# State-space scan in a two-block model: where in the program, and into which PSUM bank, each group's scores are written

## The chip, the cores and the metric

The kernel runs on one core of a Trainium2 chip. Its time is the device time of one execution in microseconds (us). A core has a matrix engine (TensorE, "PE" in the profile, with its weight loads as "PEld"), a vector engine (VectorE, "DVE"), a scalar engine (ScalarE, "ACT"), a slower general engine (GpSimd, "POOL") and a queue that issues transfers (SyncE, "SP"). Each engine works through its own instructions in the order of the program and meets the others only at semaphores. TensorE writes its results into PSUM, a memory of eight banks of 128 x 512 fp32 values; the other memory on the core is SBUF.

## The reference, cut to what matters

Two blocks of a language model are computed one after the other for 256 positions of width 1024. The second block begins with a state-space mixer of 32 heads in 8 groups of 4, head width 64, state width 128. The change is inside its scan, which in the reference is this:

```python
def ssd_chunked_scan(xs, dt, A, Bm, Cm):
    ...
    def step(state, inp):
        xc, dtc, bc, cc = inp
        cum = jnp.cumsum(dtc * A, axis=1)
        seg = cum[:, :, None] - cum[:, None, :]
        decay = jnp.exp(jnp.where(causal, seg, -jnp.inf))
        cb = jnp.einsum('btgn,bsgn->btsg', cc, bc)          # one set of scores for each group
        w = cb[..., None] * decay * dtc[:, None]            # one set of weights for each head
        y = jnp.einsum('btsgk,bsgkp->btgkp', w, xc)
        ...
```

Around the scan stand an input projection (of which the gate z is a part), a short convolution, and behind it a gate, a norm for each group and an output projection:

```python
SSD_N_HEADS, SSD_N_GROUPS, SSD_D_STATE, SSD_HEAD_DIM = 32, 8, 128, 64
zxbcdt = x @ in_proj
z = zxbcdt[..., :SSD_D_INNER]                               # 256 x 2048
```

The kernel does not carry a state between two chunks of 128: it computes the scores, the decay and the sum over all 256 positions at once, as the lower triangle of three 128 x 128 tiles (384 columns, `TRI`).

## The kernel before, in words

**Matrix products.** Every weight matrix comes in units of 1 MB (128 x 2048 fp32). SyncE loads a unit into one of five slots of `raw`; ScalarE rounds it into `whi` (L774), VectorE forms the rest `wlo` (L1201), and TensorE computes each product as three: high by high (L1938), high by low (L1939), low by high (L1940). A unit's slot is free again when TensorE has gone through it (`unit_used`).

**The stage of the scan.** It has 16 units: eight of the gate's projection (`zz`, two for each quarter of 512 columns) and eight of the output projection (`so`). Each unit is cut into four steps (`SSD_PER_UNIT`), so that there are 64 steps. In `a_unit` the function `between(n)` is called ahead of each step, and then six matmuls of 128 x 512 of the unit follow. What else belongs to a step is in the table `SSD_STEPS`: "head" h, "norm" and "yT" of a quarter of eight heads, "tail", or nothing. Heads 0 to 7 are steps 4 to 11, heads 8 to 10 steps 12 to 14, head 11 step 17, "yT" 0 is step 19, heads 12 to 18 are steps 20 to 26, head 19 is step 29, "yT" 1 step 31, head 20 step 32, head 27 step 41, "yT" 2 step 43, heads 28 to 31 steps 44 to 47, and "yT" 3 step 55.

**One head.** SyncE loads the head's row of cumulated decay into one of four buffers (`dec`, three of which lie in `arena`; `decay_row`, L641) once TensorE has finished head h - 4 (the semaphore `ssd_y`). GpSimd adds the causal mask (L735), ScalarE takes the exponential (L1026, L1027), VectorE multiplies it with the scores of the head's group in PSUM (L1745; "multiply h" below), and two steps later TensorE multiplies the product with the head's input (L2440 to L2442; "sum h" below) into the banks 2 and 3.

**The scores.** `ssd_scores` (L2429, L2430) computes a group's scores, two matmuls, at the step of the first of its four heads (0, 4, 8, ...), behind sum h - 2 and ahead of the step's six matmuls. All groups use bank 1. `claim` lets TensorE wait until the bank's last reader is done with it. For a group that is the multiply of the fourth head of the group before; where a "yT" lies between, it is that one's last reader.

**A quarter of eight heads.** When sum 8q + 7 is done, VectorE adds the banks 2 and 3 to y (L1700), multiplies with the gate (L1708), takes statistics (L1714, L1717), GpSimd the inverse root (L682), VectorE scales (L1725, "norm"). At "yT" TensorE transposes the quarter's y, eight transposes into two banks (L2460): the first half (j = 0) into bank 0 and the second (j = 1) into bank 1. ScalarE reads them (L801) and rounds them into `r_hi`, VectorE reads them (L1233) and forms `r_lo`, and the last of VectorE's reads of a half frees its bank. At a step with n = 3, VectorE's own list has the forming of a unit's `wlo` (L1201) ahead of what else the step holds, "yT" included.

**What sets the order.** All of this is written out by hand. The function `plan` walks through the same steps and notes for each use of a bank (`small`, `gemm`, `named`) which use came before it there; the waits of `claim`, `wait_bank` and `wait_drained` are made from it. VectorE's and ScalarE's lists (from L1728 and L1010) follow the same table `SSD_STEPS`.

Of the kernel before, what the change touches and what calls it, by code (L numbers as in the profile page):

```python
# [40 lines left out]
P = 128  # L41
T = 256
# [17 lines left out]
TRI = 3 * P  # L60
# [5 lines left out]
SSD_UNITS, SSD_PER_UNIT = 16, 4  # L66


def ssd_steps():

    steps = [("none", 0)] * SSD_PER_UNIT
    for h in range(SSD_HEADS):
        steps.append(("head", h))
        if h % 8 == 2 and h > 8:
            steps += [("none", 0), ("norm", h // 8 - 1)]
        if h % 8 == 3 and h > 8:
            steps += [("none", 0), ("yT", h // 8 - 1)]
    steps.append(("tail", SSD_HEADS))  # L80
    steps += [("none", 0)] * (SSD_PER_UNIT * (SSD_UNITS - 2) - 1 - len(steps)) + [("yT", 3)]
    return steps + [("none", 0)] * (SSD_PER_UNIT * 2)


SSD_STEPS = ssd_steps()


def group_order(groups):
# [119 lines left out]
def plan(w):  # L208

    p = Plan()  # L210
    w_in = w["w_in"][0]
    p.transposes("h1", 4, (4, 5, 6, 7))
    SQ, SK, SV, RET, CB, CC, CH, GATE = (MIX * j for j in (3, 4, 5, 6, 0, 1, 2, 10))
# [135 lines left out]
    for u in range(SSD_UNITS):  # L349
        c, k = u // 2, u % 2  # L350
        if c < 4:
            p.unit(("zz", c, k), w_ssd, 4 * k, 4, 512 * c, 512)
        else:
            p.unit(("so", c - 4, k), w["ssd_out_proj_2"][0], 4 * (c - 4), 4, 512 * k, 512)
        for what, h in SSD_STEPS[SSD_PER_UNIT * u:SSD_PER_UNIT * (u + 1)]:
            if what == "head":
                if h % 4 == 0:
                    p.small(("CB", h // 4), 1)
            if h % 8 == 7 and what != "yT":
                for t in range(NT):  # L360
                    p.named(("y", h // 8, t), 2 + t, "ssd_y", h + 1)
            if what == "yT":
                for b in range(2):
                    p.small(("yT", h, b), b)
        if u == 0:
            p.small(("xsN", 7), 5)
        if c < 4 and k == 1:
            for t in range(NT):
                p.gemm(("zz", c, t), ("zz", c, 1), (6, 4)[c % 2] + t)
# [86 lines left out]

def build(nc, w, out):
    plan_ = plan(w)
    use, at, units = plan_.use, plan_.at, plan_.units
    ctx = ExitStack()  # L460
    with ctx:
# [81 lines left out]
        bcT, xsN, szN = room(0, 16, T), room(4096, NT, INNER), room(8192, NT, INNER)  # L543
# [1378 lines left out]
        def _(pe):  # L1922
            M = nc.tensor.matmul
            halves_normed = [0]

            def claim(key):

                b, n, _ = use[key]
                if n:
                    pe.wait_ge(drained[b], n)  # L1930
                return bank[b]

            def fill(key):
                return filled[use[key][0]]
# [157 lines left out]
            for name in ("sq", "sk"):  # L2092
                for j in range(2):
                    b_unit(at[(name, j)], h_hi, h_lo, one((name, j)), ready=xT_ready("h1") if (name, j) == ("sq", 0) else None)
                    if (name, j) == ("sk", 1):

                        pe.wait_ge(pv_in, 176)
                        b = claim("pv0")
# [3 lines left out]
                        b = claim("pv1")  # L2102
# [8 lines left out]
            for k in range(14):  # L2111
# [4 lines left out]
                if k < SB_HEADS:  # L2116
                    b = claim(("z", k))
# [3 lines left out]
                if 1 <= k <= SB_HEADS:  # L2121

                    pe.wait_ge(sb_l_ready, k)
                    b = claim(("bet", k - 1))
                    M(b[:, 0:TRI], negu, sb_l, start=True, stop=False)
                    M(b[:, P:T], neg1, sb_l[:, T:TRI], start=False, stop=True).then_inc(fill(("bet", k - 1)), 1)
                if 2 <= k <= SB_HEADS + 1:
# [5 lines left out]
                    b = claim(("sbo", i // 4)) if i % 4 == 0 else bank[7]  # L2133
# [14 lines left out]
            for n in range(3):  # L2148
                for hf in range(2):
                    for g in range(3):  # L2150
                        if step == 1:

                            pe.wait_ge(q_rot, 4)
                            for j in range(4):
                                b = claim(("rT", j))
# [5 lines left out]
                        head = step - 2  # L2161
# [3 lines left out]
                        if 0 <= head < RET_HEADS:  # L2165
                            b = claim(("rs", head))
# [16 lines left out]
                        if step == 11:  # L2183
                            pe.wait_ge(ret_out, 2)
                            for j in range(2):
                                b = claim(("retT", j))
# [41 lines left out]
            for k in range(XA_HEADS + 3):  # L2228
                if k < XA_HEADS:
                    b_unit(at[("xq", k)], r_hi, r_lo, one(("xq", k)), ready=None if k else xT_ready("h2"))  # L2230
                if 1 <= k <= XA_HEADS:
# [3 lines left out]
                    b = claim(("xs", i))  # L2235
# [4 lines left out]
                if 2 <= k <= XA_HEADS + 1:  # L2240
                    i = k - 2
                    pe.wait_ge(xa_p, 2 * i + 2)
                    b = claim(("xp", i))
# [4 lines left out]
                if k >= 3:  # L2248
# [6 lines left out]
                    b = claim(("xo", i))  # L2255
# [125 lines left out]
            for j in range(1, 8):  # L2381
                if j >= 2:
                    b_unit(at[("bc", j)], h_hi, h_lo, one(("bc", j)))
                if j == 1:
                    w_hi, w_lo, kt, n = weights(at["dt"])
                    b = claim("dt")
# [6 lines left out]
                if j == 4:  # L2393
# [3 lines left out]
                    b = claim("cum")  # L2397
# [3 lines left out]
                if j == 6:  # L2401
                    wait_drained(pe, "cum")
                    b = claim("cumT")
# [17 lines left out]

            y_banks, so_banks = [], []

            def ssd_scores(h):

                if h % 4 == 0:
                    g = h // 4
                    b = claim(("CB", g))
                    M(b[:, 0:T], bcT[:, g, 0:P], bcT[:, 8 + g, :], start=True, stop=True)  # L2429
                    M(b[:, T:TRI], bcT[:, g, P:T], bcT[:, 8 + g, P:T], start=True, stop=True).then_inc(fill(("CB", g)), 1)  # L2430

            def ssd_y_of(h):

# [10 lines left out]
            def ssd_step(n):  # L2444
                what, h = SSD_STEPS[n]
                if what == "head":
                    if h >= 2:
                        ssd_y_of(h - 2)
                    ssd_scores(h)
                if what == "tail":  # L2450
                    ssd_y_of(SSD_HEADS - 2)
                    ssd_y_of(SSD_HEADS - 1)
                if what == "yT":
                    pe.wait_ge(y_done, 4 * h + 4)
                    for j in range(2):
                        b = claim(("yT", h, j))
                        for ct in range(2):
                            for t in range(NT):
                                c = P * (2 * j + ct)
                                last = nc.tensor.transpose(b[:, T * ct + P * t:T * ct + P * t + P], yN[h % 2][:, t, c:c + P], ident)  # L2460
                        last.then_inc(fill(("yT", h, j)), 1)

            for u in range(SSD_UNITS):
                c, k = u // 2, u % 2
# [225 lines left out]
```

## Time and profile before

| | |
|---|---|
| runs | 1326.25, 1330.86, 1335.05 us (median 1330.86) |
| profiled execution | 1332.33 us, of which the span of the trace is 1330.5 us |
| TensorE busy | 1272.0 us (96% of the span), its weight loads 1123.7 us |
| VectorE, ScalarE, GpSimd busy | 935.1 us (70%), 671.0 us (50%), 90.3 us (7%) |
| mean granted TensorE clock | 0.988 of full speed |
| the stage of the scan | from about 693 to 840 us of the span |
| chain of waits that ended last | 79% on TensorE, 11% on VectorE, 4% on ScalarE |

A busy share is an average. TensorE's 96% say that nearly everywhere the kernel is as long as its matmuls; what a change of order in the scan does has to be read from the few places in its stage where TensorE stands still, and from what ends these waits.

### The profile page before, as it was taken

What the parts mean: (1) busy time and instruction counts of PE and PEld (TensorE: products, weight loads), DVE (VectorE), ACT (ScalarE), POOL (GpSimd) and SP (SyncE); (2) the same over time, 40 slices, a digit from 0 to 9 for tenths busy, and PEclk for the clock granted to TensorE, in tenths of its full rate; (3) what the DMA queues carried; (4) which work ended last, traced back from release to release, by engine and by line L of the source; (5) the groups of instructions that cost most, each with busy time, mean ns of one, the idle gap of its engine ahead of it and who ended that gap; (6) DMA issues with size and microseconds to landing.
All of it is one profiled execution on the core that took longest, in us unless ns stands there. A gap on an engine that the chain in (4) does not pass through costs nothing.

```text
span 1330.5 us, 18576 instructions
## 1 busy us (share of the span) xinstructions
PE 1272.0 (96%) x7671; PEld 1123.7 (84%) x7671; DVE 935.1 (70%) x1291; ACT 671.0 (50%) x828; POOL 90.3 (7%) x95
## 2 busy tenths in 40 slices
PE   6999999999999999999998988999999899999997
PEld 5878999989977888889996777888888877888886
DVE  5665857775447655576976777778878846788877
ACT  3555344444434444445765544365655454466652
POOL 4000000100000000010003342100000100100000
PEclk9999999999999999998999999999999999999999
DMA  9644645655435566636555454555554532655551
GB/s 341 199 127 127 190 144 174 223 179 199 159 107 168 193 191 193 188 121 189 166 190 161 149 168 150 178 189 190 190 190 134 196 110 81 200 191 190 190 190 52
DMA packets 159876, 228.50 MB, mean 172 GB/s; under 512 B 5525, under 2 KB 122001, under 8 KB 159664
## 3 DMA queue, kind: packets, MB, share of 16 engines
q1 hardware_dynamic: 156544, 216.68, 50.7%
q0 software_dynamic: 2960, 10.05, 2.1%
q8 instruction: 61, 1.00, 0.3%
q10 hardware_dynamic: 288, 0.59, 0.1%
q14 instruction: 23, 0.19, 0.0%
HBM read 226.20 MB, written 1.10 MB: 171 GB/s over the span
## 4 chain that ended last, share of the span: by engine, by line
PE 79%; DVE 11%; ACT 4%; issue 3%; POOL 2%; DMA 1%; POOLq 0%; DVEq 0%; SPq 0%; ACTq 0%
PE psum L1938 17%; PE psum L1939 17%; PE psum L1940 17%; PE psum L1970 12%; PE psum L1969 6%; DVE wlo L1201 2%; DVE arena L1663 2%; PE psum L1967 2%; ACT whi L774 1%; PE psum L1968 1%; DMA raw<-in_w_in 1%; POOL rstd L675 1%; POOL rstd L682 1%; PE psum L2050 1%; PE psum L2238 1%
## 5 line engine op out<-in xcount | busy, mean ns | idle before, releaser
L1201 DVE TENSOR_TENSOR wlo<-raw,whi 128x2048 fp32r<-128x2048 f32 (+3 forms) x203 | 453.9, 2248 | 123.4 <-ACT whi L774 122.9
L774 ACT ACTIVATE whi<-raw 128x2048 fp32r<-128x2048 f32 (+3 forms) x203 | 378.0, 1876 | 29.1 <-DMA raw<-in_w_in 13.4
L1970 PE MATMUL psum<-h_both,whi 128*128 128x512 f32 x714 | 254.6, 396 | 0.0
L1938 PE MATMUL psum<-h_both,whi 128*128 128x256 f32 x720 | 206.6, 287 | 2.8 <-DVE h_both L1213 2.8
L1939 PE MATMUL psum<-h_both,whi 128*128 128x256 f32 x720 | 205.3, 285 | 0.0
L1940 PE MATMUL psum<-h_both,wlo 128*128 128x256 f32 x720 | 205.2, 285 | 0.0
L1969 PE MATMUL psum<-h_both,wlo 128*128 128x256 f32 x714 | 199.4, 279 | 0.3 <-DVE h_both L1233 0.3
L1938 PE MATMUL psum<-whi,r_hi 128*128 128x512 f32 (+1 forms) x464 | 181.3, 391 | 4.2 <-DVE r_lo L1616 1.7
L1939 PE MATMUL psum<-wlo,r_hi 128*128 128x512 f32 (+1 forms) x464 | 178.3, 384 | 0.0
L1940 PE MATMUL psum<-whi,r_lo 128*128 128x512 f32 (+1 forms) x464 | 178.3, 384 | 0.0
L1970 PEld LDWEIGHTS psum<-h_both,whi 128*128 128x128 f32 x714 | 134.0, 188 | 27.5
L1938 PEld LDWEIGHTS psum<-h_both,whi 128*128 128x128 f32 x720 | 139.8, 194 | 3.5 <-DVE wlo L1201 3.2
L1939 PEld LDWEIGHTS psum<-h_both,whi 128*128 128x128 f32 x720 | 139.7, 194 | 0.2
L1940 PEld LDWEIGHTS psum<-h_both,wlo 128*128 128x128 f32 x720 | 139.7, 194 | 0.0
L1969 PEld LDWEIGHTS psum<-h_both,wlo 128*128 128x128 f32 x714 | 134.6, 189 | 5.2 <-DVE h_both L1233 0.6
L1938 PE MATMUL psum<-whi,h_both 128*128 128x512 f32 (+4 forms) x352 | 129.5, 368 | 1.3 <-issue 0.9
L1939 PE MATMUL psum<-wlo,h_both 128*128 128x512 f32 (+4 forms) x352 | 125.0, 355 | 0.0
L1940 PE MATMUL psum<-whi,h_both 128*128 128x512 f32 (+4 forms) x352 | 124.7, 354 | 0.0
L1776 DVE SCALAR_TENSOR_TENSOR arena<-arena,pv 128x256 f32<-128x256 f32 x176 | 77.4, 482 | 51.8 <-ACT arena L1055 43.9
L791 ACT ACTIVATE arena<-psum 128x512 f32<-128x512 f32 (+3 forms) x83 | 44.5, 558 | 123.7 <-PE psum L1940 108.6
L1938 PEld LDWEIGHTS psum<-whi,r_hi 128*128 128x128 f32 x464 | 87.6, 189 | 20.9 <-issue 4.0
L1940 PEld LDWEIGHTS psum<-whi,r_lo 128*128 128x128 f32 x464 | 87.5, 189 | 17.7
(301 smaller groups left out, 1791.7 us busy)
## 6 DMA issues: line engine op xcount, KB each, us to landing
raw<-in_ffn_up SPq DMA_DIRECT2D x44, 1024.0 KB, 5.1
raw<-in_w_in SPq DMA_DIRECT2D x32, 1024.0 KB, 5.6
raw<-in_ssd_in_proj SPq DMA_DIRECT2D x24, 1024.0 KB, 5.4
raw<-in_ffn_down SPq DMA_DIRECT2D x22, 1024.0 KB, 4.8
raw<-in_w_up SPq DMA_DIRECT2D x16, 1024.0 KB, 5.5
raw<-in_w_down SPq DMA_DIRECT2D x16, 1024.0 KB, 5.0
raw<-in_w_xkv SPq DMA_DIRECT2D x8, 1024.0 KB, 5.4
raw<-in_ssd_out_proj SPq DMA_DIRECT2D x8, 1024.0 KB, 5.0
```

The lines of the kernel that those rows point to most:

```text
L675: nc.gpsimd.tensor_tensor(rstd[:, t:t + 1], ms[:, t:t + 1], mhalf[:, t:t + 1], ALU.pow).then_inc(rstd_ready, 1)
L774: A(whi[u % SLOTS][:, 0:kt * n], raw[u % SLOTS][:, 0:kt * n], ACT.Copy).then_inc(hi_split, 1)
L791: A(dst, src(b), ACT.Copy).then_inc(drained[use[key][0]], 1)
L1201: V.tensor_tensor(wlo[s][:, 0:kt * n], raw[s][:, 0:kt * n], whi[s][:, 0:kt * n].bitcast(F32), ALU.subtract).then_inc(lo_split, 1)
L1663: ins = V.scalar_tensor_tensor(y, spad[m % 2][:, ct, tap:tap + T], pv[:, 32 * tap + tile + ct:32 * tap + tile + ct + 1], y, ALU.mult, ALU.add)
L1776: ins = V.scalar_tensor_tensor(y, fpad[g % 2][x][:, ct, tap:tap + T], pv[:, wcol:wcol + 1], y, ALU.mult, ALU.add)
L1938: M(o, a_hi, b_hi, start=start, stop=False)
L1939: M(o, a_hi, b_lo, start=False, stop=False)
L1940: return M(o, a_lo, b_hi, start=False, stop=stop_)
L1967: M(b[:, :], w_hi_k, h_both[:, :, k, :], start=True, stop=False)
L1969: M(b[:, 0:T], w_lo_k, h_hi[:, k, :], start=False, stop=False)
L1970: return M(b[:, :], w_hi_k, h_both[:, :, k, :], start=False, stop=k == kt - 1)
```

## The change: the step and the bank of the scores

The two matmuls of a group's scores are issued at the end of the step before that of the group's first head, behind what that step holds and ahead of its six matmuls: scores 0 at step 3, and the others at the steps 7, 11, 19, 23, 31, 35 and 43, three of which (19, 31, 43) are the steps of "yT" 0, 1 and 2. Even groups use bank 0 and odd groups bank 1. The two halves of "yT" change banks: the first half goes to bank 1, the second to bank 0. So scores 3, 5 and 7 follow in bank 1 on the first half of the "yT" issued just ahead of them. The number of instructions on each engine stays, and the lists of the other engines are the same but for the banks and semaphores that they name.

```diff
--- before.py
+++ after.py
@@ -85,6 +85,12 @@
 SSD_STEPS = ssd_steps()
 
 
+def scores_after(n):
+
+    what, h = SSD_STEPS[n + 1] if n + 1 < len(SSD_STEPS) else ("none", 0)
+    return h // 4 if what == "head" and h % 4 == 0 else None
+
+
 def group_order(groups):
 
     order = [("up", 1), ("down", 0)]
@@ -352,16 +358,16 @@
             p.unit(("zz", c, k), w_ssd, 4 * k, 4, 512 * c, 512)
         else:
             p.unit(("so", c - 4, k), w["ssd_out_proj_2"][0], 4 * (c - 4), 4, 512 * k, 512)
-        for what, h in SSD_STEPS[SSD_PER_UNIT * u:SSD_PER_UNIT * (u + 1)]:
-            if what == "head":
-                if h % 4 == 0:
-                    p.small(("CB", h // 4), 1)
+        for n in range(SSD_PER_UNIT * u, SSD_PER_UNIT * (u + 1)):
+            what, h = SSD_STEPS[n]
             if h % 8 == 7 and what != "yT":
                 for t in range(NT):
                     p.named(("y", h // 8, t), 2 + t, "ssd_y", h + 1)
             if what == "yT":
                 for b in range(2):
-                    p.small(("yT", h, b), b)
+                    p.small(("yT", h, b), 1 - b)
+            if scores_after(n) is not None:
+                p.small(("CB", scores_after(n)), scores_after(n) % 2)
         if u == 0:
             p.small(("xsN", 7), 5)
         if c < 4 and k == 1:
@@ -2421,13 +2427,11 @@
 
             y_banks, so_banks = [], []
 
-            def ssd_scores(h):
-
-                if h % 4 == 0:
-                    g = h // 4
-                    b = claim(("CB", g))
-                    M(b[:, 0:T], bcT[:, g, 0:P], bcT[:, 8 + g, :], start=True, stop=True)
-                    M(b[:, T:TRI], bcT[:, g, P:T], bcT[:, 8 + g, P:T], start=True, stop=True).then_inc(fill(("CB", g)), 1)
+            def ssd_scores(g):
+
+                b = claim(("CB", g))
+                M(b[:, 0:T], bcT[:, g, 0:P], bcT[:, 8 + g, :], start=True, stop=True)
+                M(b[:, T:TRI], bcT[:, g, P:T], bcT[:, 8 + g, P:T], start=True, stop=True).then_inc(fill(("CB", g)), 1)
 
             def ssd_y_of(h):
 
@@ -2446,7 +2450,6 @@
                 if what == "head":
                     if h >= 2:
                         ssd_y_of(h - 2)
-                    ssd_scores(h)
                 if what == "tail":
                     ssd_y_of(SSD_HEADS - 2)
                     ssd_y_of(SSD_HEADS - 1)
@@ -2459,6 +2462,8 @@
                                 c = P * (2 * j + ct)
                                 last = nc.tensor.transpose(b[:, T * ct + P * t:T * ct + P * t + P], yN[h % 2][:, t, c:c + P], ident)
                         last.then_inc(fill(("yT", h, j)), 1)
+                if scores_after(n) is not None:
+                    ssd_scores(scores_after(n))
 
             for u in range(SSD_UNITS):
                 c, k = u // 2, u % 2
```

Around head 8, TensorE's list before is this. L2440 to L2442 are sum 6 and, at the end, the first matmul of sum 7; L2429 and L2430 are scores 2, and the L1938 to L1940 between are the six matmuls of step 12.

```order
L2440 MATMUL psum<-arena 128x64 [waits s_w,lo_split]
L2441 MATMUL psum<-arena 128x64
L2442 MATMUL psum<-arena 128x64
L2429 MATMUL psum<-arena 128x256 [waits drained1]
L2430 MATMUL psum<-arena 128x128
L1938 MATMUL psum<-whi0,h_both 128x512
L1939 MATMUL psum<-wlo0,h_both 128x512
L1940 MATMUL psum<-whi0,h_both 128x512
L1938 MATMUL psum<-whi0,h_both 128x512
L1939 MATMUL psum<-wlo0,h_both 128x512
L1940 MATMUL psum<-whi0,h_both 128x512
L2440 MATMUL psum<-arena 128x64 [waits drained1]
```

With the change (all lines from L1938 on are 3 to 6 further down) it begins with the end of sum 5, and the scores stand one step earlier, ahead of sum 6 and of the six matmuls that are now between sum 5 and sum 6:

```order
L2446 MATMUL psum<-arena 128x64
L2433 MATMUL psum<-arena 128x256 [waits drained0]
L2434 MATMUL psum<-arena 128x128
L1944 MATMUL psum<-whi4,h_both 128x512
L1945 MATMUL psum<-wlo4,h_both 128x512
L1946 MATMUL psum<-whi4,h_both 128x512
L1944 MATMUL psum<-whi4,h_both 128x512
L1945 MATMUL psum<-wlo4,h_both 128x512
L1946 MATMUL psum<-whi4,h_both 128x512
L2444 MATMUL psum<-arena 128x64 [waits s_w,lo_split]
```

The scores moved ahead by one step and wait for the other bank. Behind sum 6 the six matmuls of the next unit now follow at once.

Around "yT" 0, TensorE's list before has the eight transposes (L2460), the six matmuls of step 19, sum 10 (L2440 to L2442) and then scores 3:

```order
L2460 MATMUL psum<-cst,arena 128x128 [waits drained1]
L2460 MATMUL psum<-cst,arena 128x128 x3
L1938 MATMUL psum<-whi1,h_both 128x512
L1939 MATMUL psum<-wlo1,h_both 128x512
L1940 MATMUL psum<-whi1,h_both 128x512
L1938 MATMUL psum<-whi1,h_both 128x512
L1939 MATMUL psum<-wlo1,h_both 128x512
L1940 MATMUL psum<-whi1,h_both 128x512
L2440 MATMUL psum<-arena 128x64 [waits s_w,lo_split]
L2441 MATMUL psum<-arena 128x64
L2442 MATMUL psum<-arena 128x64
L2429 MATMUL psum<-arena 128x256 [waits drained1]
```

With the change (the transposes are L2463):

```order
L2463 MATMUL psum<-cst,arena 128x128 [waits drained1,y_done]
L2463 MATMUL psum<-cst,arena 128x128 x3
L2463 MATMUL psum<-cst,arena 128x128 [waits drained0]
L2463 MATMUL psum<-cst,arena 128x128 x3
L2433 MATMUL psum<-arena 128x256 [waits drained1]
L2434 MATMUL psum<-arena 128x128
L1944 MATMUL psum<-whi1,h_both 128x512
L1945 MATMUL psum<-wlo1,h_both 128x512
L1946 MATMUL psum<-whi1,h_both 128x512
```

The scores (L2433) stand directly behind the transposes and wait for bank 1, into which the first four of these transposes have just written. The six matmuls and sum 10, which stood between, are behind them.

## Rows read from the trace of the kernel before

**Rows 1.** Busy time by stretch: from:to, length, busy of each engine, PEclk, DMA share.

```profile
720.00:730.00 10.00, 6.56 (x29) 5.45 (x28) 5.95 (x9) 4.20 (x7) 3.94 (x3) 0.83 0.46 144
```

**Rows 2.** Waits in TensorE's list, 690 to 830: us in total, times, longest.

```profile
PE psum L2429 <- DVE arena L1745: 3.7, 3, 1.7
PE psum L2429 <- DVE r_lo L1233: 3.4, 2, 2.3
```

**Rows 3.** Timeline of TensorE, head 8: start, us, instruction, [idle before <-releaser].

```profile
721.83 0.41 PE L2440 MATMUL psum<-arena 128*128 128x64 f32 x2 [1.71 <-DVE arena L1745]
...
724.40 1.22 PE L2429 MATMUL psum<-arena 128*128 128x256 f32 x2 [1.72 <-DVE arena L1745]
...
728.14 0.33 PE L2440 MATMUL psum<-arena 128*128 128x64 f32 x2
...
730.38 0.41 PE L2440 MATMUL psum<-arena,dec 128*128 128x64 f32 x2
```

**Rows 4.** Timeline of TensorE, sum 13, sum 14, scores 4, sum 15, undisturbed.

```profile
752.61 0.33 PE L2440 MATMUL psum<-arena 128*128 128x64 f32 x2
...
754.68 0.33 PE L2440 MATMUL psum<-arena 128*128 128x64 f32 x2
...
755.29 0.65 PE L2429 MATMUL psum<-arena 128*128 128x256 f32 x2
...
757.38 0.33 PE L2440 MATMUL psum<-arena 128*128 128x64 f32 x2
```

**Rows 5.** Timeline of VectorE, multiply 7 (its first row) to "yT" 0.

```profile
723.80 0.55 DVE L1745 TENSOR_TENSOR arena<-arena,psum 128x384 f32<-128x384 f32 x1
...
728.95 1.28 DVE L1700 TENSOR_TENSOR arena<-arena,psum 128x512 f32<-128x512 f32 x2 [2.24 <-PE psum L2442]
...
737.64 1.62 DVE L1725 TENSOR_SCALAR arena<-arena,rstd 128x256 f32<-128x256 f32 x4 [0.94 <-POOL rstd L682]
...
740.83 2.28 DVE L1201 TENSOR_TENSOR wlo<-raw,whi 128x2048 fp32r<-128x2048 f32 x1
743.03 1.65 DVE L1233 SCALAR_TENSOR_TENSOR r_lo<-psum,pv,r_hi 128x256 fp32r<-128x256 f32 x4
```

**Rows 6.** Timeline of TensorE, "yT" 0, scores 3, sum 11.

```profile
739.31 1.12 PE L2460 MATMUL psum<-cst,arena 128*128 128x128 f32 x8 [0.52 <-DVE arena L1725]
...
744.74 1.12 PE L2429 MATMUL psum<-arena 128*128 128x256 f32 x2 [2.30 <-DVE r_lo L1233]
...
748.49 0.33 PE L2440 MATMUL psum<-arena 128*128 128x64 f32 x2
```

**Rows 7.** Timeline of TensorE, "yT" 1, sum 19, and sum 23 (the last row).

```profile
771.06 1.12 PE L2460 MATMUL psum<-cst,arena 128*128 128x128 f32 x8 [2.98 <-DVE arena L1725]
...
777.71 0.33 PE L2440 MATMUL psum<-arena 128*128 128x64 f32 x2
...
788.43 0.33 PE L2440 MATMUL psum<-arena 128*128 128x64 f32 x2
```

**Rows 8.** Timeline of VectorE, "yT" 1, multiply 21 and multiply 23.

```profile
773.59 1.65 DVE L1233 SCALAR_TENSOR_TENSOR r_lo<-psum,pv,r_hi 128x256 fp32r<-128x256 f32 x4
...
778.26 0.56 DVE L1745 TENSOR_TENSOR arena<-arena,psum 128x384 f32<-128x384 f32 x1 [1.13 <-ACT arena L1027]
...
785.67 0.54 DVE L1745 TENSOR_TENSOR arena<-arena,psum 128x384 f32<-128x384 f32 x1
```

**Rows 9.** Timeline of GpSimd, the masks of heads 26 and 31.

```profile
790.04 0.74 POOL L735 TENSOR_TENSOR arena<-arena,cst 128x256 f32<-128x256 f32 x1 [3.02 <-DMA arena<-decay_rows]
...
809.88 2.69 POOL L735 TENSOR_TENSOR arena<-arena,cst 128x256 f32<-128x256 f32 x1 [1.52 <-DMA arena<-decay_rows]
```

**Rows 10.** Timeline of TensorE, "yT" 2, sum 27, sum 31.

```profile
799.57 1.12 PE L2460 MATMUL psum<-cst,arena 128*128 128x128 f32 x8 [0.46 <-DVE arena L1725]
...
805.95 0.33 PE L2440 MATMUL psum<-arena 128*128 128x64 f32 x2
...
814.05 0.43 PE L2440 MATMUL psum<-arena 128*128 128x64 f32 x2 [1.13 <-DVE arena L1745]
```

## The prediction, written before the changed kernel ran

> **What bounds the kernel now.** I read the page first, for TensorE's share (96%, the table above): outside the scan nothing that the change touches has a wait to give back. Then the busy time by stretch: in ten of the scan's microseconds TensorE is busy for 6.56 only, at 0.83 of its full clock [rows 1]. Then who waits for whom in TensorE's list: the scores (L2429) stand for 3.7 us behind VectorE's multiplies and for 3.4 us behind its `r_lo` [rows 2]. These 7.1 us, 0.5% of the span, are all that the edit aims at. The rest had to be read in order of time, because each of TensorE's waits here ends with a VectorE instruction, and those wait in turn for ScalarE, for rows of decay or for TensorE. I call "lead" how much earlier than before TensorE reaches the same piece of work, and carry it from place to place.
>
> **The units of the sum** come from a stretch without waits [rows 4]. From sum 13 to sum 14 is 2.07 us, a sum takes 0.61 (754.68 to 755.29), so six matmuls take 1.46. Scores with six matmuls take 2.09, so scores take 0.63. Behind a wait the same scores and six matmuls took 3.74 us (724.40 to 728.14) [rows 3], in a stretch in which the granted clock was partly the lower of its two levels, 1.2 instead of 2.4 GHz (its mean is 0.83) [rows 1]. A half-speed spell behind a wait so costs 1.65 us.
>
> **What is added and removed.** No instruction is added. The sixteen score matmuls cost the same wherever they stand, and the swap of the "yT" banks costs nothing by itself: in both kernels the second half of "yT" 0, for instance, waits for the multiply of head 11, the last reader of scores 2, since it has their bank either way. Scores 0, one step earlier, wait for nothing near them. No transfer is issued at another place of SyncE's list, but SyncE and GpSimd follow TensorE's progress, so a row of decay moves with the sum that frees its buffer.
>
> **Head 4.** Scores 1 lose their part of the 3.7 us [rows 2] (1.72 is that of scores 2 [rows 3], and 2.0 is left for scores 1 and 6). It buys nothing: sum 6 stands 1.71 us behind multiply 6 [rows 3], which is the end of a run of VectorE work, and starts at 721.83 all the same.
>
> **Head 8.** Here the change works. Scores 2 are done in the time in which TensorE waits for multiply 6 anyway. From sum 6, 721.83, one step leads to 723.90. Multiply 7 ends at 724.35 [rows 5], so sum 7 starts at 724.4, not 728.14, and sum 8 at 726.5, not 730.38: a lead of **3.9 us** (the wait of 1.72, the scores, and the half-speed spell). VectorE's addition (L1700) waits for sum 7 [rows 5]; its lead is 3.7. Behind it stand statistics, GpSimd's root and the scaling at 737.64, with a wait of 0.94 only [rows 5], and the mask of head 11, whose row is issued after the same sum 7. I let the 3.7 arrive whole at "yT" 0.
>
> **"yT" 0.** Here the change works against itself. Before, the transposes (1.12 us), six matmuls and sum 10 are done, and then scores 3 wait 2.30 us [rows 6]. Now scores 3 come directly behind the transposes and need bank 1, free when VectorE has read the first half. VectorE has a unit's `wlo` of 2.28 us ahead of that read; the first two of the four reads are done 0.83 us after 743.03 [rows 5], 4.55 us after the transposes began. So TensorE stands 4.55 - 1.12 = 3.4 us instead of 2.3, with the same matmuls behind the wait instead of inside it. From the transposes to sum 11 it was 9.18 us (739.31 to 748.49) [rows 6]. It becomes 4.55 + 3.74 (scores and six, at half speed as before) + 0.61 + 1.46 = 10.36. The lead falls by 1.2, to **2.5**.
>
> **"yT" 1.** Before, the scores found their bank free, and from the transposes to sum 19 it was 6.65 us [rows 7]. Now the wait ends at 773.59 + 0.83, which is 3.36 us after the transposes began [rows 7, 8]; with 3.74 + 0.61 + 1.46 it becomes 9.17. The lead falls by 2.5, to **0**. The six matmuls of step 31 are the last of the gate's fourth quarter. ScalarE reads that quarter, splits a unit and only then makes exponential 21, for which multiply 21 waits [rows 8]. Counted back from sum 19 at full clock (1.46 + 0.63 + 0.61), these six ended at 775.0 at the latest; now it is 771.06 - 2.5 + 3.36 + 3.74 = 775.7, so 0.7 us later or somewhat more. I take 0.9. VectorE then has work in one piece to multiply 23, which ended at 786.2 [rows 8] and now ends at 787.1. Since scores 6 no longer stand between, sum 23 starts there, not at 788.43 [rows 7]: lead **1.3**. Head 26's mask waits for its row, 3.02 us before 790.04 [rows 9], and that row follows sum 22, which has no lead. So 0 to 1.3 us arrive at "yT" 2; I take 0.7.
>
> **"yT" 2.** From the transposes to sum 27 it was 6.38 us [rows 10]. It becomes the 9.17 of "yT" 1 if the clock falls, 7.5 if not. The matmuls behind the waits of 2.30 and 2.98 us took half as long again or more (1.12 us for both of L2429, where 0.65 is the undisturbed time [rows 4, 6]); the new wait is 3.36 - 1.12 = 2.2, nearest to the 2.30, so I take 9.17. Lead 0.7 - 2.8 = **-2.1**. It is carried to the end: sum 31 waits for multiply 31, the mask of head 31 at 809.88 waits for its row [rows 9], and the row follows sum 27, so sum 31 moves from 814.05 [rows 10] to about 816.2. Behind it TensorE has `so` units in one piece.
>
> **The sum.** 3.7 - 1.2 - 2.5 + 0.7 - 2.8 = -2.1: 2.1 us slower, 1332.33 + 2.1 = 1334.4 for an execution like the profiled one. That one lies 1.5 above the median of the runs shown; on the median it is 1330.86 + 2.1 = **1333**. The bounds: if all the waits of [rows 2] and one spell went and nothing came, 7.1 + 1.65 = 8.8 us faster, 1322. If the lead of head 8 never arrived and all three "yT" cost what is above, 6.5 slower, 1337.4.
>
> **The rivals.**
>
> *The lead survives: faster.* The clock may stay up behind the new waits, since fewer waits stand ahead of them. Then "yT" 0 becomes 8.7 us long (gain 0.5), "yT" 1 7.5 (loss 0.9), "yT" 2 7.5 (loss 1.1), and with head 8 and 24 it is 3.7 + 0.5 - 0.9 + 0 to 1.3 - 1.1, 2.2 to 3.5 faster: 1327 to 1329. For it: the 3.9 us of head 8 are sure to be there at sum 8. Against it: [rows 6, 7] have their spells behind waits shorter than or like the new ones.
>
> *The three waits behind "yT" with nothing against them: slower.* Place: scores 3, 5 and 7, which wait for a read made from transposes issued just ahead of them. Price: 1.2 + 2.5 + 2.8 = 6.5 us, 1337. It decides if the scaling at 737.64 hangs on something other than sum 7, so that "yT" 0 starts at 739.3 as before. For it: the rows of decay arrive late all through the stage [rows 9]. Against it: L1700's wait of 2.24 us for sum 7 [rows 5].
>
> *Nothing moves.* TensorE's waits in the scan end with VectorE's, whose chain sets the pace, and the scores only choose which wait they stand in: 1330 to 1332. The Trainium skill, "TensorE: Matmul & The Clock Gate", section "HAM oscillation", has a case that speaks for this: adding PSUM double-buffering to its kernel gave no further gain. The row at 724.40 is against it at head 8, where the bank's reader is the releaser [rows 3].
>
> *The clock.* If each of the eight scores brought a spell of its own, it would be 8 x 1.65 = 13.2 us slower, 1344. Against it: scores 4 ran in 0.65 us [rows 4]. The Trainium skill, same page, section "A second HAM failure mode: psum-queue depth-cycling", says that cycling through PSUM banks with short idle times between groups of matmuls can make the clock swing between its two levels; [rows 1, 3] show one such spell, with one bank only.
>
> **Chances and range.** The forecast (1331.5 to 1336) 0.42, the lead survives 0.27, nothing moves 0.15, the waits alone 0.13, the clock 0.03. Runs of the kernel before spread over 8.8 us, and the median of three may be off by 3. From 1325 to 1339 covers the first four cases but for their ends. One per cent is 13.3 us, about what a measurement can tell from no change; the 8.8 us of the best bound do not reach it, the clock's case would just do so: faster 0.01, within 0.96, slower 0.03.
>
> **What would show it.** Head 8: sum 8 about 3.9 us ahead of 730.38, and no half-speed scores 2. "yT" 0: L2433 with an idle time of about 3.4 us or a little more ended by VectorE's `r_lo`. "yT" 1 and 2: the same with 2.2 to 2.5 us; the two together had 3.4 - 2.3 = 1.1 before [rows 2, 6]. Sum 31 two microseconds late. The prediction is wrong if VectorE's `wlo` moves behind the reads' place in time, if the waits for L1745 outweigh these, or if sum 31 comes before 814.

## The result and the profile after

| | before | changed |
|---|---|---|
| median of 8 runs | 1330.67 us | 1341.15 us |
| lowest to highest | 1326.25 to 1335.05 us | 1337.86 to 1343.85 us |
| ratio | | 1.0082, 95% interval 1.0067 to 1.0097 |
| profiled execution, span of its trace | 1332.33, 1330.5 us | 1339.68, 1337.9 us |

The change makes the kernel 10.5 us slower, where 2.1 were forecast; 1341.15 lies outside the range of 1325 to 1339. In the runs below, the kernel before was timed beside each set of kernels (medians 1329.18 to 1331.02 us), and each ratio is to these. Two executions far above all others (1405.14 us of e5_old_place, whose median without it is 1325.43, and 2514.59 us of the kernel before) count in the medians below and in no ratio.

The first part of the page has TensorE's busy time where it was, so the loss is idle time and not work:

```profile
PE 1272.4 (95%) x7671; PEld 1122.5 (84%) x7671; DVE 936.1 (70%) x1291; ACT 670.9 (50%) x828; POOL 86.0 (6%) x95
```

The busy time by stretch of the changed kernel (from:to, length, busy of PE, PEld, DVE, ACT, POOL, then the granted clock, DMA share and GB/s) shows where it stands idle:

```profile
730.00:740.00 10.00, 4.57 (x27) 3.46 (x25) 9.06 (x12) 6.25 (x11) 4.44 (x3) 0.86 0.32 121
...
770.00:780.00 10.00, 8.41 (x32) 6.98 (x32) 4.84 (x8) 4.56 (x9) 0.00 (x0) 0.59 0.05 15
...
800.00:810.00 10.00, 5.80 (x26) 4.68 (x26) 7.27 (x12) 4.74 (x9) 1.45 (x2) 0.83 0.04 14
```

Those are the stretches of "yT" 0, 1 and 2. At 770 the mean clock is 0.59, much of it at the lower level, and in the last two the DMA engines move next to nothing (0.05 and 0.04 of their time): SyncE stands still too, because TensorE frees no slot. The waits in TensorE's list from 690 to 840, which answer to [rows 2]:

```profile
PE psum L2463 <- DVE arena L1731: 8.0, 3, 4.3
PE psum L2433 <- DVE r_lo L1239: 7.3, 3, 3.5
PE psum L2444 <- DVE arena L1751: 5.2, 5, 1.7
```

The scores (now L2433) no longer wait for a multiply, and the wait for `r_lo` has gone from 3.4 to 7.3 us. On top now is the wait of the transposes (L2463) for the scaled y (L1731): 8.0 us, where [rows 6, 7, 10] have 0.52, 2.98 and 0.46, 4.0 in all. TensorE's timeline at head 8, against [rows 3]:

```profile
719.56 0.41 PE L2444 MATMUL psum<-arena 128*128 128x64 f32 x2 [1.30 <-DVE arena L1751]
...
722.55 0.43 PE L2444 MATMUL psum<-arena 128*128 128x64 f32 x2 [0.69 <-DVE arena L1751]
...
724.90 0.41 PE L2444 MATMUL psum<-arena,dec 128*128 128x64 f32 x2
```

These are sums 6, 7 and 8. From sum 6 to sum 8 it is 5.3 us instead of 8.55. And at the three "yT", against [rows 6, 7, 10]: transposes, scores, and the second sum behind them, for each of the three, and then sum 31 and the transposes of "yT" 3:

```profile
735.25 1.12 PE L2463 MATMUL psum<-cst,arena 128*128 128x128 f32 x8 [1.90 <-DVE arena L1731]
739.89 1.22 PE L2433 MATMUL psum<-arena 128*128 128x256 f32 x2 [3.53 <-DVE r_lo L1239]
...
746.04 0.33 PE L2444 MATMUL psum<-arena 128*128 128x64 f32 x2
...
770.11 1.97 PE L2463 MATMUL psum<-cst,arena 128*128 128x128 f32 x8 [4.27 <-DVE arena L1731]
773.56 1.22 PE L2433 MATMUL psum<-arena 128*128 128x256 f32 x2 [1.48 <-DVE r_lo L1239]
...
779.93 0.33 PE L2444 MATMUL psum<-arena 128*128 128x64 f32 x2
...
802.07 1.12 PE L2463 MATMUL psum<-cst,arena 128*128 128x128 f32 x8 [1.87 <-DVE arena L1731]
805.52 1.22 PE L2433 MATMUL psum<-arena 128*128 128x256 f32 x2 [2.33 <-DVE r_lo L1239]
...
811.32 0.33 PE L2444 MATMUL psum<-arena 128*128 128x64 f32 x2
...
821.43 0.43 PE L2444 MATMUL psum<-arena 128*128 128x64 f32 x2 [1.72 <-DVE arena L1751]
...
833.34 1.04 PE L2463 MATMUL psum<-cst,arena 128*128 128x128 f32 x8
```

Each stretch from transposes to that sum is a difference of two starts: 10.8, 9.8 and 9.25 us, before 9.2, 6.65 and 6.4. L2433 takes 1.22 us each time, where 0.65 is undisturbed [rows 4]: the clock is at its lower level behind each of the waits.

The two traces are compared by the lead, counted from sum 0 (at 705.35 before and 702.80 now: the two executions differ by 2.55 us ahead of all this, which is not the change's: e5_old_place, with the changed kernel's lists up to there, has sum 0 at 704.74). Negative is later than before:

| at | forecast | measured |
|---|---|---|
| sum 8 | 3.9 | 2.9 |
| "yT" 0 | 3.7 | 1.5 |
| sum 11 | 2.5 | -0.1 |
| "yT" 1 | 2.5 | -1.6 |
| sum 19 | 0 | -4.8 |
| sum 23 | 1.3 | -3.5 |
| "yT" 2 | 0.7 | -5.1 |
| sum 27 | -2.1 | -7.9 |
| sum 31 | -2.1 | -9.9 |
| "yT" 3 | -2.1 | -11.5 |

Behind "yT" 3 the executions differ by 1.5 us the other way, so the spans are 7.4 us apart. By the medians it is 10.5: the profiled execution of before was 1.7 above its median, that of the changed kernel 1.5 below.

### The profile page after: what moved, and what is told of

The parts are those of the page before. It is cut to its first block, busy times and chain, and to the rows that moved or that the text cites. A ratio compares the mean times of both kernels' runs of the same rounds, so it can differ in the third digit from the quotient of the medians.

```text
span 1337.9 us, 18575 instructions
## 1 busy us (share of the span) xinstructions
PE 1272.4 (95%) x7671; PEld 1122.5 (84%) x7671; DVE 936.1 (70%) x1291; ACT 670.9 (50%) x828; POOL 86.0 (6%) x95
## 4 chain that ended last, share of the span: by engine, by line
PE 79%; DVE 10%; ACT 3%; DMA 3%; issue 3%; POOL 2%; POOLq 0%; DVEq 0%; SPq 0%; ACTq 0%
PE psum L1944 17%; PE psum L1946 17%; PE psum L1945 17%; PE psum L1976 12%; PE psum L1975 6%; DVE wlo L1207 2%; DVE arena L1669 2%; PE psum L1973 2%; DMA arena<-decay_rows 2%; PE psum L1974 1%; ACT whi L780 1%; POOL rstd L681 1%; DMA raw<-in_w_in 1%; POOL rstd L688 1%; PE psum L2056 1%
```

## The experiments

Line numbers in the diffs are left out. "The changed kernel" is the one predicted.

**Two theories.** A: the longer wait stands ahead of a unit's last six matmuls, so beside the wait itself the slot comes free late, and the next weights go out right ahead of the rows of decay. B: only TensorE's own standing still counts. The first run moves the scores behind the six matmuls at the three "yT" steps:

```diff
 def ssd_step(n):
     what, h = SSD_STEPS[n]
+    if n and SSD_STEPS[n - 1][0] == "yT" and scores_after(n - 1) is not None:
+        ssd_scores(scores_after(n - 1))
 ...
-    if scores_after(n) is not None:
+    if scores_after(n) is not None and what != "yT":
         ssd_scores(scores_after(n))
```

> The changed kernel, but at the three steps of "yT" 0, 1 and 2 the scores go behind the step's six matmuls, not ahead of them (still ahead of the next sum). Banks and all else stay. Theory A (late release): the wait for r_lo stands ahead of the last six matmuls of the units 4, 7 and 10, so their slots come free late, the next 1 MB of weights is issued right ahead of the rows of decay, and the rows, their masks and exponentials are late after each wait. Then this edit gives back the six matmuls' time of each wait and the late rows as well: 9 to 13 us less than the changed kernel, 1328 to 1332 us. Theory B (the wait alone): only the time that TensorE stands counts; the six matmuls cover 1.5 to 2.4 us of each of the three waits, 4.5 to 7 us in all: 1334 to 1337 us.

Measured: 1330.49 us, ratio 0.9987 (0.9972 to 1.0002), 10.7 us less than the changed kernel. That is A's range and more than B expected. The second run keeps TensorE's list and delays the weights:

```diff
 if u >= SLOTS:
     sp.wait_ge(unit_used, u - SLOTS + 1)
+zz = at[("zz", 0, 0)]
+if u - zz in (9, 12, 15):
+    sp.wait_ge(ssd_y, {9: 11, 12: 19, 15: 27}[u - zz])
```

> As the run before (six matmuls ahead of the scores at the three "yT" steps), but SyncE also holds the weights that follow the release of the units 4, 7 and 10 until sum 10, 18 and 26 are done, so that these 1 MB transfers are issued right ahead of the next rows of decay, as in the changed kernel. TensorE's list is that of the run before. Theory A (late release): rows 14, 22 and 30 land 5 to 6.5 us after their issue, not 3, and it is 4 to 7 us slower than the run before. Theory B (the wait alone): within 1 us of the run before, since the weights are needed several units later.

Measured: 1335.07 us, ratio 1.0032 (1.0017 to 1.0047), 4.6 us above the run before. So weights sent late cost time, although TensorE waits for no `whi` or `wlo` in the scan of either trace: the rows behind them are what comes late. GpSimd's masks of heads 30 and 31 in the trace of the first run, then of this one (start, us, [idle before <-releaser]):

```profile
805.80 0.73 POOL L741 TENSOR_TENSOR arena<-arena,cst 128x256 f32<-128x256 f32 x1 [8.90 <-DMA arena<-decay_rows]
```

```profile
810.80 1.44 POOL L744 TENSOR_TENSOR arena<-arena,cst 128x256 f32<-128x256 f32 x2 [12.14 <-DMA arena<-decay_rows]
```

And SyncE's issues ahead of them: the two rows from 802.71, 2.5 us behind the weights, in the first run; from 804.95, right behind them, in the second.

```profile
800.17 0.38 SPq L658 DMA_DIRECT2D raw<-in_ssd_out_proj  x1
802.71 2.38 SPq L647 DMA_DIRECT2D arena<-decay_rows  x2
```

```profile
804.52 0.38 SPq L661 DMA_DIRECT2D raw<-in_ssd_out_proj  x1
804.95 2.04 SPq L647 DMA_DIRECT2D arena<-decay_rows  x2
```

Row 30 is masked 3.1 us after its issue in the one and 5.9 us after it in the other. The changed kernel has the second picture: its rows go out from 810.06, right behind weights at 809.44, and the masks begin at 816.55.

```profile
816.55 1.43 POOL L741 TENSOR_TENSOR arena<-arena,cst 128x256 f32<-128x256 f32 x2 [14.68 <-DMA arena<-decay_rows]
```

But weights right ahead of a row are not new with the change. The kernel before has them too:

```profile
802.12 0.38 SPq L652 DMA_DIRECT2D raw<-in_ssd_out_proj  x1
802.73 4.35 SPq L641 DMA_DIRECT2D arena<-decay_rows  x2
...
807.63 0.73 POOL L735 TENSOR_TENSOR arena<-arena,cst 128x256 f32<-128x256 f32 x1 [4.86 <-DMA arena<-decay_rows]
```

For the first row behind "yT" 0, 1 and 2, this is how long behind the weights it goes out, and how long it then takes to its mask (us):

| kernel | behind the weights | to the mask |
|---|---|---|
| before | 0.6, 1.1, 0.6 | 4.9, 4.4, 4.9 |
| changed | 0.7, 0.9, 0.6 | 4.9, 4.7, 6.5 |
| e1_six_ahead | 4.6, 1.8, 2.5 | 3.0, 3.9, 3.1 |
| e2_six_held | 0.4, 0.4, 0.4 | 5.2, 5.4, 5.9 |

So late release tells the first run from the changed kernel and from the second. The changed kernel differs from the one before it by this only at "yT" 2, by 1.6 us. Why row 30 takes 6.5 us there and 4.9 before, with weights 0.6 us ahead in both, no run shows.

**The rows alone.** In the changed kernel, the rows are put ahead of the weights:

```diff
-rows_at.setdefault(at[("zz", 0, 0)] + SLOTS + n // SSD_PER_UNIT, []).append(h + 2)
+rows_at.setdefault(at[("zz", 0, 0)] + SLOTS + n // SSD_PER_UNIT
+                   - (n in (20, 21, 32, 33, 44, 45)), []).append(h + 2)
```

> The changed kernel with SyncE's list changed alone: at the three places the rows of decay of heads 14, 15, then 22, 23, then 30, 31 are issued ahead of the 1 MB of weights, not behind them. TensorE's list and all its waits stay. Theory A (late release): each of these rows lands about 3 us after its issue, not 5 to 6.4, and the exponentials behind them come 2 to 3 us earlier: 3 to 7 us less than the changed kernel, 1334 to 1338 us. Theory B (the wait alone): no change, 1340 to 1342 us.

Measured: 1341.29 us, ratio 1.0074 (1.0053 to 1.0095). No gain; A's number failed. The trace (of an execution 2.6 us above the median) says what happened: the delay went to the next row. Rows 14 and 15 are issued from 748.96 and the first is masked at 752.10, 3.1 us later. Then come the weights at 751.38, and row 16, issued at 753.09, is masked at 759.07, 6.0 us later.

```profile
752.10 0.73 POOL L741 TENSOR_TENSOR arena<-arena,cst 128x256 f32<-128x256 f32 x1 [13.21 <-DMA arena<-decay_rows]
755.66 1.38 POOL L741 TENSOR_TENSOR arena<-arena,cst 128x256 f32<-128x256 f32 x1 [2.84 <-DMA arena<-decay_rows]
759.07 0.72 POOL L741 TENSOR_TENSOR dec<-dec,cst 128x256 f32<-128x256 f32 x1 [2.02 <-DMA dec<-decay_rows]
```

**The length of the wait.** VectorE makes `r_lo` ahead of the unit's `wlo` at the "yT" steps of the changed kernel:

```diff
-if n == 3 and u < SSD_UNITS - 1:
+if n == 3 and u < SSD_UNITS - 1 and what != "yT":
     lo()
 ...
 if what == "yT":
     for j in range(2):
         ...
+    lo()
```

> The changed kernel with VectorE's list changed alone: at the "yT" steps it makes r_lo first and the unit's wlo (2.2 us) behind it. The scores' waits behind the transposes fall from 3.5, 1.5 to 2.3 and 2.3 us to about 1.3 us each. Theory B (the wait alone): that is 2.2 us at each of three places less, 1334 to 1336 us. Theory A (late release): the same 6.6 us and in addition earlier weights and rows, 1331 to 1334 us. If wlo itself becomes what TensorE waits for (the next unit's), it is above 1336 us, with a wait for lo_split in TensorE's list.

Measured: 1340.77 us, ratio 1.0076 (1.0052 to 1.01): no gain, though the waits in the trace shrank from 7.3 to 4.0 us. What grew is the wait for the normed rows (L1350) behind the scan, 3.4 us with a longest of 2.5, where the kernel before has 1.9 and 0.9:

```profile
PE psum L2434 <- DVE r_lo L1239: 4.0, 3, 1.5
PE psum L2057 <- DVE xn L1350: 3.4, 2, 2.5
```

At "yT" 3 VectorE now stands idle for ScalarE's `r_hi`, with units and the layer norm queued behind it:

```profile
832.20 1.66 DVE L1239 SCALAR_TENSOR_TENSOR r_lo<-psum,pv,r_hi 128x256 fp32r<-128x256 f32 x4 [3.44 <-ACT r_hi L807]
```

A later run leaves that step as it was (`h == 3` keeps `lo()` ahead):

> The changed kernel with r_lo ahead of wlo at "yT" 0, 1 and 2, and not at "yT" 3. In e4_rlo_first the scan was shorter in the trace by 4.4 us, and TensorE's wait for xn (L1350) behind it was 3.4 us, not 1.9. If "yT" 3 was what gave the gain back (there VectorE waits for ScalarE's r_hi with the wlo behind it, just ahead of the layer norm), this is 1336 to 1339 us. If the shorter waits are worth nothing in themselves, it stays at 1340 to 1342 us.

Measured: 1337.27 us, ratio 1.0051 (1.0036 to 1.0067). With the fourth place left alone, the three shorter waits are worth 3.9 us against the changed kernel (the two intervals meet at 1.0067). Against the run before it is 3.5 us, and those intervals overlap, so what "yT" 3 costs is likely and not clear of noise.

**Which places lose.** Four runs take the change apart. First the three scores alone go back behind their sum:

```diff
 if h >= 2:
     ssd_y_of(h - 2)
+if SSD_STEPS[n - 1][0] == "yT":
+    ssd_scores(h // 4)
 ...
-if scores_after(n) is not None:
+if scores_after(n) is not None and what != "yT":
     ssd_scores(scores_after(n))
```

> The changed kernel, but scores 3, 5 and 7, those at the steps of "yT" 0, 1 and 2, stand where they stood before: behind the next sum. Scores 0, 1, 2, 4 and 6 stay one step early, the banks stay. Theory A (the loss is made at the three "yT" places alone, by the wait and what it delays): all of the loss is gone, 1327 to 1331 us, and with the first half's bank no wait there is over 1.5 us. Theory C (the early scores cost something at every place, or the swap of the banks does): it stays above 1334 us.

Measured: 1326.13 us, ratio 0.9968 (0.9954 to 0.9983): **15.0 us** less than the changed kernel, and faster than the kernel before. Then the other half of the change, a list `EARLY` of the groups that are issued one step early, here (3, 5, 7):

```diff
+EARLY = (3, 5, 7)
 ...
-if scores_after(n) is not None:
+if scores_after(n) in EARLY:
     ssd_scores(scores_after(n))
 ...
+if h % 4 == 0 and h // 4 not in EARLY:
+    ssd_scores(h // 4)
```

> The other half of the change: only scores 3, 5 and 7 are issued one step early (behind the transposes), all others stand behind their sum as before; banks as in the change. Theory A: all of the loss and none of the gain at heads 8 and 24: 1341 to 1345 us. Theory C: the loss is shared by the places, 1334 to 1338 us.

Measured: 1342.43 us, ratio 1.0085 (1.0064 to 1.0105). And with `EARLY = ()`, the banks alone:

> Only the banks are changed (even groups 0, odd groups 1, the halves of "yT" swapped), no score moves. The waits for the multiply of the head before (3.7 us in all) go, those for r_lo shrink by the second half's 0.8 us. Theory A: 1326 to 1331 us, the banks alone cost nothing. Theory C with the banks as its cause: above 1334 us.

Measured: 1326.96 us, ratio 0.9974 (0.9962 to 0.9987). The three moved scores cost 15 us with or without the others (1342.43 - 1326.96 and 1341.15 - 1326.13). The five other moves are worth about 1 us (1326.96 - 1326.13), which is inside both intervals. The new banks are worth 3 to 4 us by themselves (1330.08 - 1326.96, or 0.26%). At "yT" 0 they shorten the wait for `r_lo` to 1.52 us, and the clock stays up behind it (L2436 takes 0.70 us, where [rows 6] have 1.12):

```profile
736.58 1.12 PE L2468 MATMUL psum<-cst,arena 128*128 128x128 f32 x8 [0.49 <-DVE arena L1734]
...
741.23 0.70 PE L2436 MATMUL psum<-arena 128*128 128x256 f32 x2 [1.52 <-DVE r_lo L1242]
...
743.37 0.33 PE L2447 MATMUL psum<-arena 128*128 128x64 f32 x2
```

The first run with `r_lo` ahead of `wlo`, at all four "yT" and then at three:

> Run e1_six_ahead with VectorE making r_lo ahead of the unit's wlo at the "yT" steps. In e1 the scores behind "yT" still wait 2.2, 0 and 1.0 us. If r_lo sets what follows, these go: 1326 to 1330 us. If it is as in e4_rlo_first, where the waits shrank and the time did not (the late wlo, or the lower clock, takes its place), it is 1330 to 1333 us.

> Run e8_six_rlo (six matmuls, then the scores, at the three "yT" steps; r_lo ahead of wlo) without the edit at "yT" 3. In e8 the scan ended 4.6 us earlier than before, by the trace, and the kernel was 1.1 us faster. If "yT" 3 gave it back: 1324 to 1327 us. If not: 1328 to 1330 us.

Measured: 1328.96 us, ratio 0.9992 (0.9978 to 1.0006), and 1326.6 us, ratio 0.9972 (0.9958 to 0.9987). "yT" 3 seems to have its price here too, 2.4 us, but these intervals overlap as well. For the kernel of e5_old_place, in which no score waits for `r_lo`, the order at the three steps adds nothing that can be told from noise: 1327.17 us, ratio 0.996 (0.9942 to 0.9979).

> Run e5_old_place (scores 3, 5 and 7 behind the sum, the others early) with r_lo ahead of wlo at "yT" 0, 1 and 2. No score waits for r_lo there, so TensorE gains nothing directly; only mask, exponential and multiply work that stands behind r_lo in VectorE's list could move. 1325 to 1328 us if r_lo was not on the path; under 1324 us if the order of VectorE's list there matters by itself.

**Where a lead goes.** In the changed kernel sum 7 has a lead of 3 us and "yT" 0 one of 1.5. Theory D: VectorE takes a quarter's statistics behind multiply 10, 18 or 26, and that multiply waits for its exponential and so for its row of decay. The edit swaps the two:

```diff
 if h > 8 and h % 8 == 1:
     add_sums(q - 1)
+if h > 8 and h % 8 == 2:
+    group_inverse = group_stats(q - 1)
 dve.wait_ge(s_exp, h + 1)
 ...
-if h > 8 and h % 8 == 2:
-    group_inverse = group_stats(q - 1)
```

> Run e10_old_rlo_three with VectorE taking a quarter's statistics ahead of multiply 10, 18 and 26, not behind them. Theory D: the lead won at head 8 is lost before "yT", because the statistics stand behind a multiply that waits for its row of decay (mask 10 at 22.5 us behind sum 0, however early sum 7 was), and the norm behind the statistics. Then "yT" starts 0.5 to 1.5 us earlier each time and the kernel is 1 to 3 us under e10_old_rlo_three. If the norm waits for something else (GpSimd's root behind mask 11, 19, 27), within 1 us of it.

Measured: **1320.05 us**, ratio 0.9916 (0.9893 to 0.9939), 7 us under its neighbour without the edit by the medians, 6 by the ratios. The direction was D's, the size twice or more the 1 to 3 us that D had expected. The same edit in three more kernels:

> The changed kernel with the statistics ahead of multiply 10, 18 and 26, nothing else. The three waits for r_lo stay. If the lead lost between the places hangs on the multiply ahead of the statistics (theory D), as in e12_old_stats (7.1 us under its neighbour), it is 1334 to 1338 us. If the waits at "yT" are all of the loss, and the statistics count only where these are gone, 1339 to 1342 us.

> The kernel before with the same edit alone. Theory D: here too the norm of a quarter hangs on multiply 10, 18 and 26: 1325 to 1329 us. If only a kernel with a lead at heads 8, 16 and 24 can use it, 1329 to 1332 us.

> Run e5_old_place with the statistics ahead of the multiplies, and wlo ahead of r_lo as in the change. With e12_old_stats it tells what the order of r_lo and wlo adds. Theory D: 1318 to 1322 us, as e12, since no score waits for r_lo.

Measured: the changed kernel with it 1334.95 us, ratio 1.0041 (1.0029 to 1.0054), 6.2 us less; the kernel before 1326.63 us, ratio 0.9973 (0.9959 to 0.9986); e5_old_place with it 1322.21 us, ratio 0.9933 (0.9912 to 0.9953), 3.9 us less. By the ratios the three gains are 5.5, 3.6 and 4.7 us. VectorE's list of the last one, with the statistics (L1720) between the gate (L1714) and multiply 10 (L1753):

```profile
726.34 1.83 DVE L1714 TENSOR_TENSOR arena<-arena 128x512 f32<-128x512 f32 x2
728.20 1.41 DVE L1720 BATCH_NORM_STATS2 bn<-arena 128x6 f32<-128x256 f32 x4
...
730.33 0.55 DVE L1753 TENSOR_TENSOR arena<-arena,psum 128x384 f32<-128x384 f32 x1
730.80 2.28 DVE L1207 TENSOR_TENSOR wlo<-raw,whi 128x2048 fp32r<-128x2048 f32 x1
733.01 1.61 DVE L1731 TENSOR_SCALAR arena<-arena,rstd 128x256 f32<-128x256 f32 x4
```

The scaling (L1731) follows `wlo` without the idle 0.94 us of [rows 5]: GpSimd's root is done while VectorE is still busy. Its rows in the kernel before and in this one:

```profile
734.58 3.03 POOL L682 TENSOR_TENSOR rstd<-ms,mhalf 128x4 f32<-128x4 f32 x1 [1.87 <-DVE ms L1257]
```

```profile
730.49 1.04 POOL L688 TENSOR_TENSOR rstd<-ms,mhalf 128x4 f32<-128x4 f32 x1 [1.73 <-DVE ms L1263]
```

In all thirteen traces without the edit the root of each of the first three quarters begins 0.16 us behind the start of a `wlo` on VectorE (734.41 before) and takes 3.0 us, and the scaling waits 0.91 to 0.94 us for it behind `wlo`. In the four with the edit multiply 10, 18 or 26 stands between the statistics and `wlo`, so the root begins 0.3 us ahead of `wlo`, takes 1.0 us, and nobody waits for it. Why it takes 3.0 us beside `wlo` the runs do not show. So the edit has two effects, which no run separates. The root gives 0.9 us at each of three places, 2.8 in all. D's wait, of the multiply for its exponential, is 2.20, 1.14 and 1.47 us in the trace of e10_old_rlo_three, 4.8 in all, but 0.32, 0.28 and 0.32 in the changed kernel and nothing in the kernel before. That is 7.6 us for the 6 to 7 of e12_old_stats, 3.7 for the 5.5 to 6.2 of the changed kernel, and 2.8 for the 2.5 to 3.6 of the kernel before, which owes its gain to the root alone as far as the traces tell.

The three moved scores cost 12.7 us even with the edit (1334.95 - 1322.21), so this is a second effect beside them and no explanation of them.

## Why the prediction was wrong

The direction and the place were right, the size was not.

- **The waits at "yT"** were sized almost as they came out. The stretches grew by 1.6, 3.2 and 2.9 us, 7.7 in all, where 1.2 + 2.5 + 2.8 = 6.5 were forecast; the lower clock was there each time.
- **"I let the 3.7 arrive whole at 'yT' 0"** is the step that failed first. Sum 7 had 3.0, "yT" 0 had 1.5. The prediction took the VectorE work between the two as long as before and without a new wait. Counted from sum 0, the addition (L1706) has a lead of 2.9 us, and then the gate (L1714) takes 1.83 us where it had 1.29, multiply 10 waits 0.32 us for its exponential where it had no wait, and the scaling (L1731) takes 2.08 us where it had 1.62: 1.3 us of the 1.4 that are gone at the transposes. In the trace two masks of GpSimd now run beside the gate, where there was none, and two beside the scaling, where there was one; that they are the cause is not shown. Between sum 23 and "yT" 2, another 1.5 us are lost, 1.3 of them by the same three (1.83, 0.32 and 2.07 us for 1.29, 0 and 1.62). The 3.9 us of head 8 are mostly there at sum 8 (2.9), but e5 against e7 leaves about 1 us of all five early scores in the kernel's time.
- **"It is carried to the end"** is the step that cost most: from sum 27 to "yT" 3, 3.6 us more were lost, where I had nothing. The prediction let a late row shift by as much as the sum that frees its buffer. But row 30 takes 6.5 us from its issue to its mask instead of 4.9, and multiplies 30 and 31 with a `wlo` between them follow it in one piece: 2.0 us are lost up to sum 31. Sum 31 then waits 1.72 us with the lower clock behind it, where the 1.13 us of [rows 10] had none, and that is the other 1.5. I had not followed SyncE's list through at this place. That a row takes longer with weights closer ahead of it is what e1 and e2 show, and over three places it is worth 4.6 us there; why it took longer here than before, with the weights as close in both, stays open.
- **The sum across places.** From "yT" 0 to "yT" 3 the lead fell by 13 us; 7.7 are the stretches at "yT", 3.6 the end, and the rest is 1.5 to 1.6 each ahead of "yT" 1 and 2 less 1.2 won back at head 24. Ahead of "yT" 1 it is multiply 17, which waits 1.71 us for its exponential, 0.25 before. Against the kernel with the same banks the moved scores cost 15 us, and the traces have not been added up to that.
- **"The swap of the banks costs nothing by itself"** was wrong in the kernel's favour: it gains 3 to 4 us (e7). By luck this made the miss smaller.
- **The rivals.** The slower one had the right place (scores 3, 5 and 7) and priced it at 6.5 us, with "yT" 0 starting no earlier as its condition. Measured against the kernel with the same banks it is 15. "The lead survives" and "Nothing moves" are refuted: the interval of 1.0067 to 1.0097 leaves out both. The clock was no rival of its own: scores 1, 2, 4 and 6 brought no spell. The Trainium skill's case in which adding PSUM double-buffering gave no further gain ("TensorE: Matmul & The Clock Gate", section "HAM oscillation") is not this one: here two banks in the old places bring 0.26% (e7).

## What to carry to other kernels

Before issuing work earlier, look at what it will wait for in its new place: a wait for a read of something that TensorE itself has just written is not removed by another bank, and it needs other work of TensorE's between the two. Ask also what stands behind the wait: if it holds the last use of a buffer, a large transfer starts late, and small urgent ones can come right behind it. And a lead is worth only what the next in-order list lets through: here a multiply ahead of the statistics, and a root that began just behind a `wlo` and not just ahead of it, cost 2.5 to 7 us, depending on the kernel.

## What was not expected of the hardware

In the four kernels of the table above, a row of 192 KB reached its mask 3.0 to 3.9 us after its issue when the last 1 MB of weights had gone out 1.8 us or more ahead of it, and 4.4 to 6.5 us after it when that was 0.4 to 1.1 us; row 16 of e3_rows_first took 6.0 us with weights 1.7 us ahead. An instruction of GpSimd on 128 x 4 elements took 3.0 us when VectorE had begun a `wlo` of 2.28 us just ahead of it, and 1.0 us when it began 0.3 us before that. The clock did not fall behind a wait of 1.52 us (L2436 above). Behind the 1.48 us of "yT" 1 the matmuls ran at the lower level, but so had the transposes ahead of that wait (1.97 us, where it is 1.12 at "yT" 0), behind 4.27 us of idle time: the single wait does not tell.

The fastest kernel found is that of e12_old_stats: two banks, scores 3, 5 and 7 behind their sums, `r_lo` ahead of `wlo` at three steps, statistics ahead of the multiply. It takes 1320.05 us, 0.8% less than the kernel before and 21 us less than the changed one; e15_place_stats, at 1322.21, cannot be told from it.
